# A two-layer SSD and attention backbone with routed experts: earlier loads of the first experts' weights, the last tile's rows written before the last routing part, and filler products around the last transposes

## The reference

```python
xl = xl + g1 * yl                                  # mixer output, gated
hl2 = modulate(rmsnorm(xl, norm2_g[i]), sh2, sc2)  # "normed rows"
scores = sigmoid(hf @ router_w)                    # router, all rows
# best group of 4 experts by its top-2 biased scores, then top-2 inside it
u = silu(hf @ w_gate[e]) * (hf @ w_up[e])
out = out + combine[:, e:e + 1] * (u @ w_down[e])
```

## Time and profile before

| | |
|---|---|
| median of 3 runs | 1394.73 us (1390.72 to 1395.54) |
| profiled execution | 1397.84 us, span of its instructions 1395.70 us |
| mean granted TensorE clock | 0.977 |
| TensorE busy | 1303.9 us, 93% of the span |
| VectorE busy | 548.5 us, 39% |
| ScalarE busy | 372.8 us, 27% |
| GpSimd busy | 214.8 us, 15% |
| DMA | 358.52 MB, mean 257 GB/s |
| chain that ended last | TensorE 72%, DMA 15%, VectorE 8%, ScalarE 2% |

### The profile page before, as it was taken

The page is one execution under the profiler, slowest core; times in us unless marked ns, Lnnn a source line. Parts: engine busy times, 40 slices in busy tenths (PEclk is TensorE's granted clock), DMA queues, the critical chain, the costliest instruction groups (busy, mean ns, idle before and its releaser), DMA issues.

```text
span 1395.7 us, 13590 instructions
## 1 busy us (share of the span) xinstructions
PE 1303.9 (93%) x5279; PEld 619.1 (44%) x5279; DVE 548.5 (39%) x889; ACT 372.8 (27%) x706; POOL 214.8 (15%) x206
## 2 busy tenths in 40 slices
PE   5899999999999999969999999999998989988987
PEld 3344444444444445644344333444445574332432
DVE  1456656656556042632111111753429471111113
ACT  2336565766765000100010000310136210000000
POOL 1002243443443100010000001212102100000001
PEclk9999999999999999979999999999999989999999
DMA  9233676576656700489999999930000859999996
GB/s 362 79 124 121 223 260 216 186 289 223 234 195 229 286 20 15 159 329 361 430 427 427 427 428 394 382 115 0 1 15 0 309 191 425 425 428 427 427 428 254
DMA packets 77802, 358.52 MB, mean 257 GB/s; under 512 B 9530, under 2 KB 27626, under 8 KB 62370
## 3 DMA queue, kind: packets, MB, share of 16 engines
q1 hardware_dynamic: 67643, 326.16, 59.1%
q0 software_dynamic: 4528, 16.31, 3.1%
q10 hardware_dynamic: 5564, 15.16, 2.8%
HBM read 343.70 MB, written 13.90 MB: 256 GB/s over the span
## 4 chain that ended last, share of the span: by engine, by line
PE 72%; DMA 15%; DVE 8%; ACT 2%; issue 1%; SPq 1%; ACTq 1%; POOL 0%; DVEq 0%; POOLq 0%
PE psum L1633 21%; PE psum L2293 10%; PE psum L770 10%; PE psum L781 8%; PE psum L1115 6%; DMA ring<-in_moe_w_up 6%; DMA ring<-in_moe_w_down 5%; PE psum L299 3%; PE psum L2345 2%; DMA arena<-moe_h_d,arena 2%; PE psum L814 2%; PE psum L834 1%; DMA arena<-mod_d 1%; PE psum L830 1%; PE psum L1396 1%
## 5 line engine op out<-in xcount | busy, mean ns | idle before, releaser
L1633 PE MATMUL psum<-ring,arena 128*64 128x512 f32 (+1 forms) x1344 | 411.7, 606 | 23.5 <-DMA ring<-in_moe_w_down 9.8
L1633 PEld LDWEIGHTS psum<-ring,arena 128*64 128x64 f32 (+1 forms) x1344 | 147.6, 153 | 258.6 <-issue 221.3
L770 PE MATMUL psum<-hT,ring 128*128 128x512 f32 x384 | 169.7, 596 | 0.0
L2293 PE MATMUL psum<-ring,hT 128*128 128x512 f32 x320 | 138.9, 593 | 0.0
L1115 PE MATMUL psum<-ring 128*128 128x512 f32 x256 | 113.8, 602 | 2.4 <-ACT ring L929 1.3
L781 PE MATMUL psum<-hT,ring 128*128 128x512 f32 x256 | 112.5, 592 | 0.0
L770 PEld LDWEIGHTS psum<-hT,ring 128*128 128x128 f32 x384 | 71.3, 190 | 91.3 <-issue 91.3
L975 DVE SCALAR_TENSOR_TENSOR arena<-arena,cols 128x512 f32<-128x512 f32 x96 | 92.8, 967 | 3.4
L2293 PEld LDWEIGHTS psum<-ring,hT 128*128 128x128 f32 x320 | 60.1, 190 | 73.0 <-issue 72.2
L1747 ACT ACTIVATE arena<-psum 128x512 f32<-128x512 f32 x20 | 12.0, 598 | 250.1 <-PE psum L1633 250.1
L913 ACT ACTIVATE ring<-ring,dts 128x128 f32<-128x128 f32 x256 | 76.5, 387 | 0.5
(11 more groups left out here) (346 smaller groups left out, 1489.5 us busy)
## 6 DMA issues: line engine op xcount, KB each, us to landing
ring<-in_moe_w_down SPq DMA_DIRECT2D x30, 2048.0 KB, 22.0
ring<-in_moe_w_gate SPq DMA_DIRECT2D x28, 2048.0 KB, 19.9
ring<-in_moe_w_up SPq DMA_DIRECT2D x26, 2048.0 KB, 18.1
arena<-in_ada_w SPq DMA_DIRECT2D x60, 512.0 KB, 6.0
ring<-in_ssd_w_in SPq DMA_DIRECT2D x16, 1024.0 KB, 6.9
ring<-acs_d SPq DMA_DIRECT2D x16, 1024.0 KB, 6.9
ring<-in_da_w_in SPq DMA_DIRECT2D x6, 2048.0 KB, 16.8
ring<-in_ada_w SPq DMA_DIRECT2D x20, 512.0 KB, 4.8
```

The costliest lines, as they stand in the source:

```text
L770: mm = pe.matmul(psum[:, bank, :], w_[:, k, c0:c0 + P], hT[:, k, :], start=(k == 0), stop=(k == KD - 1))
L1633: mm = pe.matmul(psum[rows, dst, :], lhsT[:, k, rows], slot(s_, a)[:, k, part], start=(k == 0), stop=(k == a - 1))
L2293: mm = pe.matmul(psum[:, 4 + m_ % 2, :], hT[:, k, t * P:(t + 1) * P], slot(qkv_slot[n], KD)[:, k, :], start=(k == 0), stop=(k == KD - 1))
```

## The change

It has four parts.

- SP's wait for the two `row_stored` semaphores ahead of the third first load of layer 0 is taken out. The wait for `wo_mm` at 8 stays.
- In both layers `tile_out` of the last tile stands ahead of the last part of `route_vector` on VectorE, not behind it.
- In both layers TensorE gets six filler calls ahead of the transposes of the last tile and three between these transposes and the last logits. Ahead of the six stands a wait for the addition that last read their PSUM bank (`wo_added` at 7, `out_added` at 3).
- The fillers between counts and one-hot product are 30 calls, not 28.

```diff
@@ wout_tensor
                 if n == 6:
                     moe0.norm.tensor(pe, (2,))
+            pe.wait_ge(wo_added, 7)
+            keep_busy(pe, 4, 6)
             moe0.norm.tensor(pe, (3,))
+            keep_busy(pe, 4, 3)
             moe0.logits_part(pe, 2)
             keep_busy(pe, 4, 10)
@@ wout_vector
+            moe0.norm.tile_out(v, TT - 1)
             moe0.route_vector(v, step, 2)
-            moe0.norm.tile_out(v, TT - 1)
@@ Moe.router_tensor
-                keep_busy(pe, 5, 28)
+                keep_busy(pe, 5, 30)
@@ att_tensor
+            pe.wait_ge(A["out_added"], 3)
+            keep_busy(pe, 5, 6)
             moe1.norm.tensor(pe, (1,))
+            keep_busy(pe, 5, 3)
             moe1.logits_part(pe, 1)
             keep_busy(pe, 5, 10)
@@ block.sync
             stored = [(moe0.row_stored[j], 16 * (TT // 2)) for j in range(2)]
-            moe0.sync_first(sp, ([(wo_mm, 7)], [(wo_mm, 7)], [(wo_mm, 8)] + stored, [], [], []))
+            moe0.sync_first(sp, ([(wo_mm, 7)], [(wo_mm, 7)], [(wo_mm, 8)], [], [], []))
@@ block.vector
+            moe1.norm.tile_out(v, LT - 1)
             moe1.route_vector(v, step, 1)
-            moe1.norm.tile_out(v, LT - 1)
             moe1.place_vector(v, step)
```

## The result

| | before | after |
|---|---|---|
| median | 1395.54 us (5 runs, 1390.72 to 1398.94) | 1385.49 us (5 runs, 1380.26 to 1386.35) |
| profiled execution | 1397.84 us, span 1395.7 | 1385.49 us, span 1383.4 |
| mean granted clock | 0.977 | 0.985 |
| TensorE busy | 1303.9 us | 1297.7 us |

The ratio is 0.992 with a 95% interval of 0.9894 to 0.9947: 10 us less. A second measurement on another occasion gave 1382.65 us against 1394.12 us, ratio 0.9921 (0.9892 to 0.9950). The forecast was 1384.4 us, 10.3 less, with a range of 1378.0 to 1391.5.

A forecast was written before the change was run, and what follows sets the result against it. Bound by the chain from routing to experts, with layer 0's gather under four weight loads, then full TensorE (layer 1 also DMA). 1.5 + 5.8 + 1.5 + 1.5 = 10.3 us off 1394.7 gives 1384.4 us; range 1378 to 1391.5.

The forecast's parts named there:

- index: Layer 0 routing: index ready earlier through early tile_out and logits at full clock; +1.5 us, ends -1.2 and +2.5.
- gather: Layer 0 gather of normed rows, no longer under four loads: 5.3 us instead of 11.08; +5.8 us, ends 0 and +7.4.
- gate product: Layer 0 transposes and first gate product, less slow clock after a shorter idle wait; +1.5 us, ends 0 and +3.9.
- layer 1: Same move and fillers in layer 1: routing, and the loads waiting for it, earlier; +1.5 us, ends +0.5 and +2.0.
- The loads: Layer 0: SP's four 2 MB loads go out 16.4 us earlier, worth nothing themselves, only in what they no longer meet.
- The row store: Layer 0: last rows' store, now under the loads, takes 10.9 us, lands at 591.7, costs nothing.
- clock drop in the new gap: Layer 0, TensorE behind the logits: gap grows from 0.9 to 2.3 us; fully slow fillers delay the one-hot product 3.7 us.
- Rival B: Layer 0: row store lands only when SP's queue has drained, 601.5; gain 3.9, 1390.8 us; chance 0.08.
- Rival D: Layer 0: row store starved between four loads, taking 32.7 us; slower, 1402.8 us; chance 0.04.
- Rival A: Layer 0: gather stays at 11 us, bound by its own 4 KB rows or small loads; 1391.2 us; chance 0.12.
- The fillers: TensorE around the last transposes: they keep the clock, so layer 0's logits end earlier; 1.5 us saved.
- The expert stages: Both layers: the stage moves with the first gate product or the routing; head start given back priced at nothing.

The follow-up runs named there:

- Loads only: Against the kernel before: only SP's wait for the row stores taken out, VectorE order and fillers as before; ratio 0.9942, 1385.54 against 1394.18 us.
- fillers only: Against the kernel before: only the new TensorE fillers and the waits ahead of them; ratio 0.9996, 1394.29 against 1394.18 us.
- moves only: Against the kernel before: only the two moves of tile_out on VectorE; ratio 0.9980, 1390.37 against 1394.18 us.
- late store: Against the changed kernel: ScalarE holds the store of the last tile's rows until the one-hot tables are ready; ratio 0.9951, 1387.84 us.
- second execution: The changed kernel profiled once more, no edit against it; 1382.65 us, ratio to before 0.9921.
- both: Against the changed kernel: six small attention loads issued ahead of the first expert loads, and more fillers behind logits and one-hot product; ratios 0.9925 and 0.9904.
- layer 1 only: Against the kernel before: only layer 1's move of tile_out and fillers, layer 0 as before; ratio 0.9983, 1393.12 against 1396.07 us.

## Why the prediction was right

The time is 1.1 us from the forecast. The four terms of the sum, taken at 1.5 (index), 5.8 (gather), 1.5 (gate product) and 1.5 (layer 1), measured 2.5, 5.7, 2.0 and 1.4 in the two traces: 11.6 us, not 10.3. The medians are 10.05 us apart, with an interval of 3.7 us to either side, so that the difference of the medians came within 0.3 us of the forecast is luck. The mechanism of the loads and the gather was right; that of the fillers in layer 0 was not.

- *The loads.* Right: they are worth the gather's contention. Loads only gives 10.5 us at load 7, fillers only 0.2, moves only 2.8. The rope table was put at 598.5, with a mark 0.93 us earlier; it landed at 599.5.
- *The row store.* 10.9 us was taken, 10.7 measured; landing 591.7 forecast, 592.1 measured. The store landed some 5 us ahead of the last two loads. The prediction held that it costs nothing only because its rows are early; with the loads alone it was issued 6.1 us later and still landed 1.7 us ahead of the gather's issue. The Trainium skill's page "DMA: Bandwidth & Descriptors", section "Queues, rings and completion order", has an engine take turns between the queues for which it has work. By that rule, which the prediction weighed, the store need not wait until SP's queue has drained, and this trace agrees. Rival B, that it lands when SP's queue has drained, is out. Rival D, that the loads starve it, is out too: 10.5 to 11.8 us in nine executions under four loads, not 32.7. What a late store costs is shown only by a store that was issued 13 us later.
- *The gather.* 5.3 us was taken from the end of layer 1, 5.35 measured. Rival A is out.
- *Index and ranking.* The best case was 2.5 us, and I took 1.5 because of a clock drop in the new gap. It measured 2.54: that gap was 2.41 us in layer 0 and the clock stayed at 1.00. In the late store, whose code is the same up to there, it fell (60 filler records in 8.57 us), and the one-hot product started 0.5 us later; in layer 1, with 2.34 us, it fell too. So a gap of this length can go either way, and a value between the ends was a fair price. Layer 1 had 1.38 us, and 1.99 in the second execution, for 1.5 taken. In layer 1 the fillers did hold back the one-hot product, by 1.1 us against before, and SP's loads did not mind, as the prediction had it.
- *The fillers.* Here the step failed: 1.5 us of the sum in layer 0 rested on one trace in which the logits were slow. They are at full clock in four of six executions without any of these fillers. And the logits at half clock cost the gather nothing: where they ran at full clock, the one-hot product ran at half, and the gather came no earlier. 2.3 to 2.5 us of the index came with loads and moves and no new filler: the move of `tile_out`, put at 1.0, had 0.9 by itself, and behind it the one-hot product ran at full clock. The prediction could not see that from one execution, but it should have held the term as a chance, not as a cost that is always paid. The index came out 1.0 us better than taken and not worse, for another reason than the one given: that is luck.
- *The first gate product.* +1.5 was taken; 0.9 (transposes) and 1.1 (gate) came. Nearly the whole 3.9 was there to be had: with both, the transposes took 1.04 us and the gate product 7.10, 3.8 us less than before.
- *The parts don't add.* Loads only has as much at load 7 as the whole change. With the index 2.5 us earlier, the gather starts just as the last loads land and takes 1 us longer (5.35 instead of 4.31). The fillers behind the one-hot product, now at full clock, end at +24.2 instead of +28.2. So TensorE idles 3.05 us instead of 0.50, and the gate product pays 1.7 us. In layer 0 the move gives back nearly all that it brings, and what remains of moves and fillers is layer 1's 1.4 to 2 us. The prediction added them.
- *The expert stages.* Right for layer 0: from load 7 to the first transposes of the next layer 261.4 to 263.6 us in all executions, for load 7 anywhere from +36 to +48.5. For layer 1, right in the changed kernel (load 7 to the landing of the down weights 208.9 and 209.3 us, 209.4 before) and where it was tested alone, but eight executions of other kernels gave back 0.6 to 2.8 us there.

## What to carry to other kernels

When a load is held back to protect a small transfer, ask what it collides with instead: here the wait protected a 0.5 MB store that had 2 to 5 us to spare, and put 8 MB beside a gather that had none. Read a price that depends on the clock from several executions before it goes into a sum. And measure the parts one by one: a step that is moved earlier into the tail of a transfer is worth less than its own time.

## What the runs showed of the hardware

- A gap of 2.3 to 2.4 us on TensorE behind the logits was followed by a granted clock of 0.50 (its lower level, 1.2 GHz) in some executions and not in others. In layer 0 the 60 filler records behind it took 6.94 us in four executions and 8.57 in one (late store). In layer 1 they took 8.35 to 9.56 us in all six executions with that gap, and 6.94 in the three where more fillers had made it 0.56 us.
- A wait of 6.1 to 7.5 us ahead of the transposes was followed by transposes of 1.97 us instead of 1.04 to 1.09 and a gate product of 8.9 to 9.9 us instead of 7.1, each time (before, moves only, fillers only, layer 1 only, late store). A wait of 2.5 to 3.05 us made the gate product 8.8 to 9.0 us in four executions of four; one of 1.2 us or less left it at 7.1 in five of five.
- A store of 0.5 MB beside four loads of 2 MB took 10.5 to 11.8 us in nine executions of six kernels, as much as beside two (10.9), and 2.6 alone. A gather of 0.5 MB took 11.1 to 11.3 us when it began 8 to 14 us behind the issue of the four loads (before, moves only, fillers only, layer 1 only), and 4.3 to 5.7 us when it began 22 us or more behind it.
- The first 570 us, which no kernel here changed, ended anywhere from 569.9 to 577.7 us. Of this spread of 7.9 us 4.6 stand already at the first product of layer 0's projection (41.6 to 46.1 us). That is why the rows here count from a mark behind it.
